# Layer 0 attention reordered around a convolution of 35 units, its row minimum fused into the score read, and layer 1's division moved ahead of the next maximum

## What is computed

```python
# layer 0: eight heads of 64 features; keys are the cached 128 and up to three neighbouring tiles
u = gc * xa;  y_a = gb * (u[t-1] * w[0] + u[t] * w[1] + u[t+1] * w[2])      # the convolution
s = q @ k.T * 64 ** -0.5      # masked outside the window
p = softmax(concat([s, sink]))[..., :-1];  y_b = p @ v
out = concat([y_a, y_b]) @ w_out

# layer 1: eight heads of 96 features, all 640 keys
s = q @ k.T * 96 ** -0.5;  p = softmax(s);  y_c = p @ v
```

## Time and profile before

| what | us |
|---|---|
| median of 3 runs (lowest, highest) | 4251.79 (4249.85, 4253.86) |
| the profiled execution's own time | 4251.46 |
| its span, first to last instruction | 4249.7 |
| layer 0's attention, in that span | 148.2 to 335.9 |
| layer 1's attention | 2280.6 to 2451.1 |

### The profile page before, as it was taken

How to read it: one execution, slowest core, us unless ns; L and a number is a source line. 1 busy time by engine, 2 the same in 40 slices (tenths; PEclk the granted TensorE clock), 3 DMA queues, 4 the chain that set the end, 5 groups by cost and what they waited for, 6 DMA issues and landing times.

```text
span 4249.7 us, 57024 instructions
## 1 busy us (share of the span) xinstructions
PE 4084.1 (96%) x19676; PEld 3440.0 (81%) x19676; DVE 2832.4 (67%) x5043; ACT 1219.2 (29%) x1744; POOL 2219.2 (52%) x1784
## 2 busy tenths in 40 slices
PE   6898999999999999999988889999999999999998
PEld 6778988888888788888776689888888888888886
DVE  7677796999114898787625448969981116666665
ACT  2233012233322233333233430122223223333332
POOL 2323447777777454444341124477777756444441
PEclk8988999999999999999999999999999999999999
DMA  5652223333346998888533511333333339888883
GB/s 212 232 207 91 69 111 128 128 126 118 120 146 194 340 355 312 312 316 315 203 131 106 183 60 65 109 127 129 127 129 123 119 122 337 303 288 290 290 286 139
DMA packets 336774, 796.94 MB, mean 188 GB/s; under 512 B 71424, under 2 KB 73184, under 8 KB 336128
## 3 DMA queue, kind: packets, MB, share of 16 engines
q1 hardware_dynamic: 175248, 500.38, 33.4%
q10 hardware_dynamic: 83568, 159.94, 10.1%
q0 software_dynamic: 77824, 134.97, 9.5%
HBM read 640.67 MB, written 154.42 MB: 187 GB/s over the span
## 4 chain that ended last, share of the span: by engine, by line
PE 92%; DVE 5%; ACT 1%; DMA 1%; issue 1%; SPq 0%; ACTq 0%; POOL 0%; DVEq 0%; POOLq 0%
PE acc L604 15%; PE acc L606 15%; PE acc L605 15%; PE aux L878 5%; PE aux L880 5%; PE aux L879 5%; PE acc L878 5%; PE acc L879 5%; PE acc L880 5%; PE acc L835 3%; PE acc L833 3%; PE acc L834 3%; PE aux L803 1%; PE aux L761 1%; PE aux L1016 1%
## 5 line engine op out<-in xcount | busy, mean ns | idle before, releaser
L573 POOL DMA_INDIRECT gate_d<-gate_v,spot_i x1024 | 1142.7, 1116 | 370.9 <-issue 341.6
L604 PE MATMUL acc<-a_hi,w_hi 128*128 128x512 f32 (+1 forms) x3248 | 1182.9, 364 | 44.0 <-DVE a_lo L1430 32.3
L605 PE MATMUL acc<-a_lo,w_hi 128*128 128x512 f32 (+1 forms) x3248 | 1171.8, 361 | 0.0
L606 PE MATMUL acc<-a_hi,w_lo 128*128 128x512 f32 (+1 forms) x3248 | 1171.7, 361 | 0.0
L604 PEld LDWEIGHTS acc<-a_hi,w_hi 128*128 128x128 f32 x3248 | 614.5, 189 | 138.2 <-issue 49.0
L605 PEld LDWEIGHTS acc<-a_lo,w_hi 128*128 128x128 f32 x3248 | 614.5, 189 | 80.6 <-issue 0.5
L606 PEld LDWEIGHTS acc<-a_hi,w_lo 128*128 128x128 f32 x3248 | 613.8, 189 | 79.9
L1665 DVE TENSOR_TENSOR w_lo<-w_in,w_hi 128x1024 fp32r<-128x1024 f32 x224 | 273.3, 1229 | 573.2 <-ACT w_hi L1203 569.9
L540 POOL DMA_INDIRECT found<-in_v,where_i x256 | 313.3, 1224 | 495.2 <-DVE total L1852 400.4
L1831 DVE TENSOR_TENSOR w_lo<-w_in,w_hi 128x1024 fp32r<-128x1024 f32 x256 | 313.0, 1224 | 225.0 <-ACT w_hi L1242 224.4
L521 POOL CAST w_hi<-w_in 128x1024 fp32r<-128x1024 f32 (+1 forms) x89 | 97.5, 1095 | 685.5 <-DMA w_in<-in_wq 230.6
(11 more groups left out here) (273 smaller groups left out, 5974.2 us busy)
## 6 DMA issues: line engine op xcount, KB each, us to landing
w_in<-in_u SPq DMA_DIRECT2D x256, 512.0 KB, 5.0
w_in<-in_v SPq DMA_DIRECT2D x256, 512.0 KB, 4.4
gate_d<-zeros ACTq DMA_DIRECT2D x32, 2048.0 KB, 8.6
act_s<-l_out ACTq DMA_DIRECT2D x256, 256.0 KB, 2.0
ag<-act_s SPq DMA_DIRECT2D x256, 256.0 KB, 4.8
ag<-gate_d SPq DMA_DIRECT2D x256, 256.0 KB, 5.9
w_in<-in_in SPq DMA_DIRECT2D x32, 512.0 KB, 5.8
w_in<-in_wq SPq DMA_DIRECT2D x32, 512.0 KB, 3.5
```

The lines of the kernel that those rows point to most:

```text
L573: pool.indirect_dma_start(gate_d[l], bass.IndirectOffsetOnAxis(ap=spot_i[:, n, k:k + 1], axis=0), gate_v[:, n, k:k + 1], None).then_inc(sp ...
L604: pe.matmul(out, wh, hi[:, k, n], start=(k == 0), stop=False)
L605: pe.matmul(out, wh, lo[:, k, n], start=False, stop=False)
L606: return pe.matmul(out, wl, hi[:, k, n], start=False, stop=(k == kt - 1))
```

## The change

It has four parts.

1. Layer 0, VectorE: the scores are kept negated. The read of the first 128 keys also accumulates the row minimum, starting from the negated sink; the read of the other keys takes that as its start and leaves the minimum over both. The separate maximum and negation are gone, and the exponential takes `scale=-1.0`. The division comes one unit sooner (u-2 in step u). The sum with the sink's exponential is made by `tensor_scalar` in place of `tensor_tensor`.
2. Layer 0, TensorE: step v is now transposes of v, values of v-1, scores of v+3, then all convolution steps of the unit in one block.
3. The 160 convolution steps go over 35 units (4 or 5 each). The pieces on VectorE follow: `conv_in`, `conv_sum`, `conv_out` now stand in steps 7 to 9, 17 to 19, 28 to 30 and 38 to 40 (before: 6 to 8, 15 to 17, 24 to 26, 33 to 35), and the parts for the output projection in steps 38 to 43 of ScalarE and 40 to 45 of VectorE, in a new order.
4. Layer 1, VectorE: step u divides unit u-1, not u-2, before it takes the maximum of unit u. ScalarE's and TensorE's order is untouched.

```diff
@@ -308,8 +309,10 @@
 
         SQ = [0, 8, 16, 24, 27, 29, 37]
 
-        CONV_FIRST, CONV_EVERY = 2, 3
-        MIXED_AT = [34, 35, 36, 37, 38, 39, 40]
+        CONV_FIRST, CONV_UNITS = 2, 35
+        CONV_PAST = [(12 - CONV_FIRST) * 16 * min(v, CONV_UNITS) // CONV_UNITS for v in range(NH * NT + 1)]
+        MIXED_AT = [38, 39, 40, 41, 42, 43]
+        MIX_ORDER = {0: (0, 1, 2, 4, 5, 6, 3, 7), 1: tuple(range(KD))}
         UNITS0 = [(j, s, b) for j in range(4) for s in range(2) for b in range(NT)]
 
         def local(b):
...
@@ -327,8 +330,9 @@
 
         def conv_done(v):
 
-            c = CONV_FIRST + v // CONV_EVERY
-            return c if v >= 0 and v % CONV_EVERY == CONV_EVERY - 1 and c < 12 else None
+            if not 0 <= v < NUNIT or CONV_PAST[v] // 16 == CONV_PAST[v + 1] // 16:
+                return None
+            return CONV_FIRST + CONV_PAST[v] // 16
 
         def keys_of(b):
             return P if b == 0 else P + local(b)[1] * P
...
@@ -764,14 +769,8 @@
                 mm.then_inc(pv_done, 1)
 
             conv = conv_steps()
+            scores_of(2)
             for v in range(NUNIT):
-                if v == 0:
-                    scores_of(2)
-                if v + 3 < NUNIT:
-                    scores_of(v + 3)
-                steps = (5, 5, 6)[v % CONV_EVERY]
-                for _ in range(3):
-                    next(conv, None)
                 pe.wait_ge(p_ready, v + 1)
                 if v >= 1:
                     pe.wait_ge(pt_ready, v)
...
@@ -779,14 +778,16 @@
                     mm = pe.transpose(aux[1][:, 0, c * P:(c + 1) * P],
                                       s_sb[:, v % 4, c * P:(c + 1) * P], ident[:])
                 mm.then_inc(pt_done, 1)
-                for _ in range(steps - 3):
-                    next(conv, None)
                 if v >= 1:
                     weigh(v - 1)
+                if v + 3 < NUNIT:
+                    scores_of(v + 3)
+                for _ in range(CONV_PAST[v + 1] - CONV_PAST[v]):
+                    next(conv)
             weigh(NUNIT - 1)
 
             def out_and_route(l):
-                by_feature_pair(OUT[l], KD * (1 + 3 * l))
+                by_feature_pair(OUT[l], KD * (1 + 3 * l), MIX_ORDER[l])
                 for k in range(2, KD):
                     by_feature(OUT[l] + k)
                 norm_total()
...
@@ -1137,17 +1138,17 @@
                     act.wait_ge(pv_done, v + 1)
                     act.activation(y[rows, 4 + j, b * P:(b + 1) * P], aux[1][rows, 1, 0:P], ACT.Copy)\
                        .then_inc(pv_read, 1)
-                if conv_done(u - 3) is not None:
-                    take_conv(conv_done(u - 3))
+                if conv_done(u - 4) is not None:
+                    take_conv(conv_done(u - 4))
                 if u < NUNIT:
                     j, s, b = UNITS0[u]
                     n, st, hd = keys_of(b), stat[:, u % 4, :], 4 * s + j
-                    act.wait_ge(neg_ready, u + 1)
+                    act.wait_ge(s_read, u + 1)
                     act.activation(s_sb[:, u % 4, 0:n], s_sb[:, u % 4, 0:n], ACT.Exp, bias=st[:, 1:2],
-                                   accum_out=st[:, 2:3])
+                                   scale=-1.0, accum_out=st[:, 2:3])
                     act.activation(st[:, 3:4], sink[:, hd:hd + 1], ACT.Exp, bias=st[:, 1:2]).then_inc(e_ready, 1)
                 if u in MIXED_AT:
-                    k = MIXED_AT.index(u)
+                    k = MIX_ORDER[0][MIXED_AT.index(u)]
                     if k == 0:
                         act.wait_ge(made, OUT[0])
                     if k < 4:
...
@@ -1163,7 +1164,7 @@
                 else:
                     act.wait_ge(gated, NT)
                 act.wait_ge(made, OUT[l])
-                for k in range(0 if l else KD - 1, KD):
+                for k in MIX_ORDER[l][0 if l else len(MIXED_AT):]:
                     act.activation(a_hi[:, k, :], y[:, k, :], ACT.Copy).then_inc(hi_ready, 1)
                 if l == 0:
                     act.wait_ge(mod_used, MODS_D.stop - (FIRST_MOD - BY_DVE))
...
@@ -1534,20 +1535,22 @@
                 note(dve.tensor_tensor(y[:, j, 0:P], y[:, j, 0:P], conv[:, 0:P], ALU.mult))
                 dve.tensor_tensor(y[:, j, P:T], y[:, j, P:T], conv[:, 130:642], ALU.mult).then_inc(conv_ready, 1)
 
-            def low_part(k, s):
-
-                dve.wait_ge(hi_ready, KD * s + k + 1)
+            def low_part(n, s):
+
+                k = MIX_ORDER[s // 3][n]
+                dve.wait_ge(hi_ready, KD * s + n + 1)
                 dve.tensor_tensor(a_lo[:, k, :], y[:, k, :], a_hi[:, k, :].bitcast(F), ALU.subtract)\
                    .then_inc(lo_ready, 1)
 
-            for u in range(NUNIT + 3):
+            step(dve.tensor_scalar(sink_n[:], sink[:], -1.0, None, ALU.mult))
+            for u in range(NUNIT + 6):
                 if u - 2 in MIXED_AT:
                     low_part(MIXED_AT.index(u - 2), 1)
-                if u >= 3:
-                    v = u - 3
+                if 2 <= u < NUNIT + 2:
+                    v = u - 2
                     n, st = keys_of(UNITS0[v][2]), stat[:, v % 4, :]
                     dve.wait_ge(e_ready, v + 1)
-                    step(dve.tensor_tensor(st[:, 4:5], st[:, 2:3], st[:, 3:4], ALU.add))
+                    step(dve.tensor_scalar(st[:, 4:5], st[:, 2:3], st[:, 3:4], None, ALU.add))
                     step(dve.reciprocal(st[:, 5:6], st[:, 4:5]))
                     dve.tensor_scalar(s_sb[:, v % 4, 0:n], s_sb[:, v % 4, 0:n], st[:, 5:6], None, ALU.mult)\
                        .then_inc(p_ready, 1)
...
@@ -1557,17 +1560,17 @@
                     dve.wait_ge(s_done, u + 1)
                     if u >= 4:
                         dve.wait_ge(pt_done, u - 3)
-                    ins = dve.tensor_scalar(s_sb[:, u % 4, 0:P], s_bank(u)[:, 0:P], SCALE_B, None, ALU.mult)
+                    low = 1 if b == 0 else 0
+                    ins = dve.tensor_scalar(s_sb[:, u % 4, 0:P], s_bank(u)[:, 0:P], -SCALE_B, sink_n[:, hd:hd + 1],
+                                            ALU.mult, ALU.min, accum_out=st[:, low:low + 1])
                     if b > 0:
-                        note(ins)
+                        step(ins)
                         skip = P * (local(b)[0] - b)
-                        ins = dve.scalar_tensor_tensor(s_sb[:, u % 4, P:n], s_bank(u)[:, P:n], SCALE_B,
-                                                       mask[:, skip:skip + n - P], ALU.mult, ALU.add)
+                        ins = dve.tensor_tensor_reduce(out=s_sb[:, u % 4, P:n], in0=s_bank(u)[:, P:n],
+                                                       in1=mask[:, skip:skip + n - P], scale=-SCALE_B,
+                                                       scalar=st[:, 0:1], op0=ALU.add, op1=ALU.min,
+                                                       accum_out=st[:, 1:2])
                     ins.then_inc(s_read, 1)
-                    dve.wait_ge(s_read, u + 1)
-                    step(dve.reduce_max(st[:, 0:1], s_sb[:, u % 4, 0:n], AX.X))
-                    dve.tensor_scalar(st[:, 1:2], st[:, 0:1], sink[:, hd:hd + 1], -1.0, ALU.max, ALU.mult)\
-                       .then_inc(neg_ready, 1)
                 for after, piece in enumerate((conv_in, conv_sum, conv_out)):
                     c = conv_done(u - 4 - after)
                     if c is not None and c % 3 == 2:
...
@@ -1578,8 +1581,8 @@
 
             def out_and_route(l):
                 s = 1 + 3 * l
-                for k in range(0 if l else KD - 1, KD):
-                    low_part(k, s)
+                for n in range(0 if l else len(MIXED_AT), KD):
+                    low_part(n, s)
 
                 def modulate_c(i):
                     modulate_next(MODS_C[i], w_mod_c[:, i % 3, :], mod_c_in[i % 3], i // 3 + 1)
...
@@ -1961,9 +1964,9 @@
                 rotate(6 + h, q_head[:, h % 2, NP_TOK:T], acc[1][0:96, 0, :], rope[0:96], 96)
 
             turn_head(0)
-            for u in range(NUNIT + 2):
-                if u >= 2:
-                    v = u - 2
+            for u in range(NUNIT + 1):
+                if u >= 1:
+                    v = u - 1
                     h, b = divmod(v, NT)
                     n, st = (P if b == 0 else T), stat[:, v % 2, :]
                     dve.wait_ge(s_read, NUNIT + v + 1)
```

20 lines of the change are left out of this document (11 added, 9 removed).

## The result

The changed kernel takes 4264.62 us (median of 8 runs, 4259.23 to 4271.45) against 4251.12 for the kernel before in the same comparison: ratio 1.0032, 95% interval 1.0023 to 1.0041. It is **13.5 us slower**. The profiled execution took 4264.56 us with a span of 4262.8, against 4251.46 and 4249.7 before, so its 13.1 us are what the trace has to account for.

A forecast was written before the change was run, and what follows sets the result against it. TensorE, busy 96% of the span, was taken as the bound; VectorE counts only where TensorE waits or runs at half clock. 4251.5 - 19 (layer 0) + 19.5 (layer 1) = 4252 us, range 4237 to 4267.

The forecast's parts named there:

- the likeliest case: Whole kernel: both layers' effects near each other, 4243.5 to 4260 us, likeliest 4252; chance 0.42.
- the clock decides: Layer 1, slower rival: each stall brings two stretches at half clock, +16 instead of 6, 4268 us; chance 0.17.
- layer 0 gains little: Layer 0, slower rival: the fused read costs twice the old, layer 0 saves 10 us, sum 4261; chance 0.12.
- the prediction's own signs of being wrong: Layer 1: values of b=1 under 5 us behind the rope turn; or layer 0: half clock before unit 35.
- Layer 1, the wait that is put in: Values of b=1 wait behind rotation, maximum, exponential and copy: 5.9 us from turn, 2.7 more in each of seven heads.
- Layer 1, what is given back: Division no longer waits for the next maximum: 0.4 us off per head, 2.5 in the last head.
- Layer 1, the clock: New idles of some 3 us bring half clock in five heads of seven, 1.3 us each: +6 us.
- TensorE's own pace: Layer 0: 2.18 us per unit and 0.44 per convolution step, 157.6 us for 40 units with 160 steps.
- the switch term: Layer 0, TensorE: one change between kinds of matmul less per unit saves 0.1 us each, 4 us in all.
- Layer 0, VectorE: Without maximum and negation, VectorE needs some 0.6 us less per large unit, about 20 us over 40 units.
- Layer 0, start and tail: TensorE idle 1.5 us at unit 0; units 35 to 39: 5 us idle, half clock costing 4 and 1.5.
- the 317: Layer 0's attention ends at 317 us, including 3 for collisions in steps 10 to 13 and 28 to 30.

The follow-up runs named there:

- `fill`: The changed kernel with three surplus 512-column score products of b=3 in seven heads of layer 1, where TensorE stood idle: 4248.9 us.
- `l1_only`: The kernel before with only layer 1's part of the change, the division one unit sooner: 4276.5 us.
- `unfused`: `rotate_behind` with layer 0's fused minimum undone (plain reads, maximum and negation back on VectorE): 4232.0 us.
- `rotate_behind`: The changed kernel with layer 1's rotation of the next head moved behind the maximum and negation of b=2, early division kept: 4228.3 us.

## Why the prediction came out as it did

The time, 4264.6, lies in the range 4237 to 4267, but the likeliest case (4252, no change) isn't what happened. What happened lies between two rivals on the slower side: the clock decides (4268, chance 0.17), which it did with 14 us where the forecast had 6 and that rival 22, and layer 0 gains little (4261, chance 0.12), which it did too, but not for the reason given there, a dear fused read. That the range held is partly luck: the two misses, +8.2 in layer 0 and +4.8 in layer 1, have the same sign, and the time lies 2.4 us under the range's upper end. One of the prediction's own signs of being wrong came: layer 0 still shows half clock before unit 35.

- **Layer 1, the wait that is put in: right.** Forecast 5.9 us from turn to values, measured 5.76; forecast 2.7 us more per head, measured 2.51. The chain was the one named: rotation, maximum, negation, exponential, copy.
- **Layer 1, what is given back: right in kind, under-sized.** Forecast 0.4 us in seven heads and 2.5 in the last, 5.3 in all. In the forecast's terms, which count the wait from the 3.25 of before, it is 7 x 2.51 + 14.3 - 24.3 = 7.6; the 11.8 above also holds the step from 3.25 to 2.66. It was read from single waits of 0.5 us in the earlier trace rows; the sum of all waits for `p_sb` over layer 1, 15.1 us in the trace of before, was not taken.
- **Layer 1, the clock: the step that failed.** "I take five falls of seven at 1.3 us": +6. It was seven of seven, three of them two stretches long, and `fill` prices them at 14.3 us, 2.0 per head; the forecast had put the point from which the clock decides at 2.1. Both idles of 3.3 us known from before had come with a fall, and the forecast gave no ground for five of seven. Still, the rows did not force seven: the idle of 1.40 in the earlier trace rows was one of six of 1.1 to 1.5 us in layer 1 of before, and the other five had none; and in `l1_only` an idle of 3.28 us had none either (last section). Why it was all seven here, and why three of them twice as long, stays open.
- **Layer 0, TensorE's own pace: right; the switch term: wrong.** Timeline of the changed kernel, transposes of units 15 and 20:

```profile
222.20 0.27 PE L778 MATMUL aux<-ident,s_sb 128*128 128x128 f32 x1
...
243.18 0.27 PE L778 MATMUL aux<-ident,s_sb 128*128 128x128 f32 x1
```

  20.98 us with 23 steps leave 20.98 - 23 x 0.44 = 10.86, 2.17 per unit, against 2.18 before. One change of kind less per unit is worth nothing; the 4 us were not there.
- **Layer 0, VectorE: right.** Groups of the changed kernel (answer to the earlier trace rows): the fused reads take 349 and 618 ns and 82 or 83 for each result, so 0.70 us for the large one where 0.60 + 0.1 were taken. The 20 us forecast for the two small passes are the 19.7 between `unfused` and `rotate_behind`.

```profile
L1564 DVE TENSOR_SCALAR_CACHE_REDUCE s_sb<-aux,sink_n 128x128 f32<-128x128 f32 x40 | 13.9, 349 | 72.8 <-PE aux L722 53.5 <-PE aux L718 19.3
L1569 DVE CUSTOM_DVE_ANT_0 s_sb<-aux,mask,stat 128x384 f32<-128x384 f32 x16 | 9.9, 618 | 0.6
...
L1564 DVE DVE_READ_ACCUMULATOR s_sb<-aux,sink_n 128x1 f32 x40 | 3.3, 82 | 0.0
```

  One line's instructions in the changed kernel, ns min/median/max: the one-column sum, the fused read, the division (answers to the earlier trace rows).

```profile
L1553 DVE TENSOR_SCALAR stat<-stat x40: 204/210/215, 150.8 to 320.7; 128x1 f32<-128x1 f32 x40
L1569 DVE CUSTOM_DVE_ANT_0 s_sb<-aux,mask,stat x32: 482/551/620, 149.6 to 314.8; 128x256 f32<-128x256 f32 x16, 128x384 f32<-128x384 f32 x16
L1555 DVE TENSOR_SCALAR s_sb<-s_sb,stat x40: 285/453/2521, 151.3 to 321.2; 128x384 f32<-128x384 f32 x16, 128x512 f32<-128x512 f32 x16, 128x128 f32<-128x128 f32 x8
```

  Neither the sum nor the fused read is ever held beside GpSimd, and the division is, up to 2521 ns: the wait stands in the sum's place, as forecast. With the rule of the Trainium skill, SBUF — State Buffer, section "Who interferes with whom", that the prediction cited, the trace agrees for the fused read and the division. The same section of the Trainium skill says: "Issue order, not op shape, decides who blocks." That is what the two timelines at unit 11 show, with 0.06 and 0.05 us between the starts. The tail of `rotate_behind` doesn't bear it out, by the starts that the trace gives: the division begins 0.04 us ahead of the split and is still the one that is stretched (in `fill` too, 0.05 ahead and 2.67 us long).

```profile
306.51 2.66 DVE L1555 TENSOR_SCALAR s_sb<-s_sb,stat 128x512 f32<-128x512 f32 x1
306.55 2.34 POOL L519 TENSOR_TENSOR w_lo<-w_in,w_hi 128x1024 fp32r<-128x1024 f32 x1
```

- **Layer 0, start and tail.** The idle at the start was 1.45 (forecast 1.5), but half clock behind it was forecast nowhere; it lasted 6.8 us and cost about half of that. The tail's idle was 3.29 + 2.23 = 5.5 (forecast 5), but for another reason than the count of VectorE's work: its first part is one division beside a split, as the timeline of the changed kernel's tail shows.

```profile
311.84 2.34 POOL L519 TENSOR_TENSOR w_lo<-w_in,w_hi 128x1024 fp32r<-128x1024 f32 x1
311.94 2.52 DVE L1555 TENSOR_SCALAR s_sb<-s_sb,stat 128x512 f32<-128x512 f32 x1
...
314.52 1.11 PE L778 MATMUL aux<-ident,s_sb 128*128 128x128 f32 x4 [3.29 <-DVE s_sb L1555]
```

  The collisions on the way cost 2.5 + 1.1 us of idle and half of another 6.8 at half clock, 7 instead of the 3 taken. Half clock in the tail lasted 10.2 us, 4.5 of them idle, so it cost about 2.9 where 5.5 were forecast. So the 317 became 325.2: +4 (switch), +3.4 (clock at the start), +4 (collisions), -2.1 (tail), which is 1 us more than measured. Of the five profiles with this layer 0, the two without a stall at unit 11 ended at 320.6 and 320.2, the others at 322.8 to 325.4: the forecast was 3 to 8 us too good, and which of these it is changes from kernel to kernel.
- **The sum.** -10.8 instead of -19 and +24.3 instead of +19.5. Both misses point the same way and share a cause, the clock: 8 us in layer 1, and 6.8 in layer 0 ahead of unit 35 (half of twice 6.8), where the prediction had none. In layer 1 the clock's +8.3 is partly made up by a wait 1.3 smaller and a gain 2.3 larger than forecast. By its own tests: values 5.76 us behind the turn, seven waits near 3 us and none for `p_sb` came out; last values near 317, heads of 23 to 24 us (they took 25.1) and half clock in layer 0's tail alone did not.

## What to carry to other kernels

When a step in a fixed order is moved, look at what stands behind its wait, not only at its own time: here the rotation took 2.0 us, and a maximum whose input was ready stood behind it and behind 1.4 us of its wait. Two edits that look like one (divide earlier; rotate earlier, because it hung on the same loop index) may have opposite signs of 12 and 36 us; take them apart before judging either. Price an idle of TensorE as wait plus clock: here 21.7 us of waiting brought 14.3 of clock, and surplus matmuls in the gap gave the 14.3 back. And compare several traces before a few us of one stage are given to an edit.
